# A streaming-encoder block on one core: k copied across partitions by GpSimd for two jobs, and six steps of the mixer put in another order

## What is computed

```python
proj = h @ w_in                       # q, k, v of 8 + 8 heads, gate, forget logits
o_sb = stick_breaking_attention(...)  # 8 heads of 64
o_fx = forgetting_attention(...)      # z = q k^T/8 + f_q - f_keys; softmax; @ v   (q, k RMS-normed)
o_sb = rmsnorm(o_sb); o_fx = rmsnorm(o_fx) * sigmoid(fox_gate)
mix  = concat([o_sb, o_fx]) @ w_out
x    = x + gate * mix
```

## Time and profile before

| | us |
|---|---|
| median of 3 runs | 1086.93 (1086.85 to 1087.13) |
| the profiled execution: time | 1086.3 |
| the profiled execution: span from first to last instruction | 1084.5 |

### The profile page before, as it was taken

One profiled execution on the slowest core, in us unless ns is written; L12 is line 12 of the kernel. 1 busy time (PEld: TensorE's weight loads), 2 busy tenths in 40 slices (PEclk: granted clock), 3 DMA queues, 4 the chain that ended last, 5 costly groups with the idle time before them and its releaser, 6 DMA issues.

```text
span 1084.5 us, 16281 instructions
## 1 busy us (share of the span) xinstructions
PE 1070.2 (99%) x6072; PEld 911.4 (84%) x6072; DVE 692.1 (64%) x1054; ACT 501.6 (46%) x834; POOL 42.3 (4%) x76
## 2 busy tenths in 40 slices
PE   8999999999999999999999999999999999999998
PEld 5788888888878889889778777789999999988886
DVE  3755555555653557886786677578776676684343
ACT  5523222222322225776796676458544544541322
POOL 1000000000000001111111011000000000000000
PEclk9999999999999999999999999999999999999999
DMA  9868888885474552397799677246786676232221
GB/s 343 240 216 289 263 277 290 268 307 161 134 229 137 167 168 78 89 218 170 177 193 187 135 146 165 61 123 156 191 218 173 172 203 183 81 108 98 88 97 78
DMA packets 209197, 191.84 MB, mean 177 GB/s; under 512 B 7676, under 2 KB 183916, under 8 KB 207084
## 3 DMA queue, kind: packets, MB, share of 16 engines
q1 hardware_dynamic: 201392, 146.59, 45.7%
q0 software_dynamic: 7424, 44.04, 16.2%
q10 hardware_dynamic: 316, 0.32, 0.1%
HBM read 186.74 MB, written 44.04 MB: 213 GB/s over the span
## 4 chain that ended last, share of the span: by engine, by line
PE 91%; ACT 3%; DMA 2%; DVE 2%; issue 1%; SPq 0%; POOL 0%; DVEq 0%; ACTq 0%
PE bank L897 28%; PE bank L899 27%; PE bank L898 27%; PE bank L1256 1%; PE bank L908 1%; PE bank L1228 1%; PE bank L1204 1%; DMA w_raw<-in_w_ffn_down_dram 1%; PE bank L1205 1%; PE bank L1291 1%; DMA x_nat<-in_x_dram 1%; ACT w_hi L1432 1%; DMA k_hh_b<-k_hh_b 0%; PE bank L934 0%; DMA k_hh_a<-k_hh_a 0%
## 5 line engine op out<-in xcount | busy, mean ns | idle before, releaser
L897 PE MATMUL bank<-h_hi,w_hi 128*128 128x512 f32 (+1 forms) x592 | 230.3, 389 | 0.1
L899 PE MATMUL bank<-h_hi,w_lo 128*128 128x512 f32 (+1 forms) x592 | 223.5, 378 | 0.0
L898 PE MATMUL bank<-h_lo,w_hi 128*128 128x512 f32 (+1 forms) x592 | 223.4, 377 | 0.0
L1939 DVE TENSOR_TENSOR w_lo<-w_raw,w_hi 128x1024 fp32r<-128x1024 f32 x97 | 118.7, 1225 | 155.9 <-ACT w_hi L1432 155.3
L1432 ACT ACTIVATE w_hi<-w_raw 128x1024 fp32r<-128x1024 f32 x97 | 102.5, 1057 | 203.8 <-PE bank L899 181.1
L897 PEld LDWEIGHTS bank<-h_hi,w_hi 128*128 128x128 f32 x592 | 111.8, 189 | 25.5 <-issue 4.2
L898 PEld LDWEIGHTS bank<-h_lo,w_hi 128*128 128x128 f32 x592 | 111.7, 189 | 24.0 <-issue 2.9
L899 PEld LDWEIGHTS bank<-h_hi,w_lo 128*128 128x128 f32 x592 | 111.6, 189 | 22.6
L2046 DVE TENSOR_TENSOR up_lo<-up_raw,up_hi 128x1024 fp32r<-128x1024 f32 x80 | 86.6, 1086 | 21.0 <-ACT up_hi L1502 21.0
L899 PE MATMUL bank<-combo,up_lo 128*128 128x256 f32 x320 | 90.6, 283 | 0.0
L897 PE MATMUL bank<-combo,up_hi 128*128 128x256 f32 x320 | 90.5, 283 | 0.0
(11 more groups left out here) (284 smaller groups left out, 2143.7 us busy)
## 6 DMA issues: line engine op xcount, KB each, us to landing
w_sums<-in_w_ffn_up_dram POOLq DMA_DIRECT2D x24, 1280.0 KB, 8.7
ada_w<-in_w_ada_dram SPq DMA_DIRECT2D x56, 512.0 KB, 3.9
w_raw<-in_w_ffn_up_dram SPq DMA_DIRECT2D x48, 512.0 KB, 6.9
up_raw<-w_sums SPq DMA_DIRECT2D x40, 512.0 KB, 5.5
w_raw<-in_w_in_dram SPq DMA_DIRECT2D x28, 512.0 KB, 4.6
w_sums<-w_sums POOLq DMA_DIRECT2D x8, 1280.0 KB, 10.0
up_raw<-in_w_ffn_up_dram SPq DMA_DIRECT2D x20, 512.0 KB, 4.1
down_raw<-in_w_ffn_down_dram SPq DMA_DIRECT2D x20, 512.0 KB, 3.6
```

The costliest lines, as they stand in the source:

```text
L897: mm(dst, wh, xh, start=start, stop=False, skip_group_check=skip)
L898: mm(dst, wh, xl, start=False, stop=False, skip_group_check=skip)
L899: return mm(dst, wl, xh, start=False, stop=stop, skip_group_check=skip)
L1939: v.tensor_tensor(w_lo[:, s, :], w_raw[:, r, :], w_hi[:, s, :].bitcast(F32), ALU.subtract)\
```

## The change

For jobs 6 and 7 `repeat_k` makes the two copies of k with GpSimd instructions instead of DMAs, and the scores wait for their own semaphore. Six pairs are added to AHEAD, which apply in this order. In the list of each engine this makes:

- `square 5` stands in front of `part 4` (ACT alone; part 4 is the output of job 2).
- `split 94` stands behind ACT's copy of `decay 6,1` and behind `unload 5,3` (ACT and DVE), in front of the first prep of job 6.
- ACT, around the start of job 7. Before: gate passes of evac 22, split 96, decay 7,1, unload 6,3, prep 7,0. After: decay 7,1, unload 6,3, gate passes of evac 22, split 96, prep 7,0.
- DVE at the same place. Before: evac 22 (sig), sum 6,4, split 96, unload 6,3, prep 7,0. After: sum 6,4, unload 6,3, evac 22, split 96, prep 7,0.
- `square 14` stands in front of the gate passes of evac 23 (ACT alone).

PE's own order is the same as before.

```diff
@@ AHEAD
     (("prep", 6, 1), ("scale", 11)),
+    (("square", 5), ("part", 4)),
+    (("split", 94), ("stat", 11)),
+    (("decay", 7, 1), ("evac", 22)),
+    (("evac", 22), ("scores", 7, 0)),
+    (("split", 96), ("prep", 7, 0)),
+    (("square", 14), ("evac", 23)),
@@ semaphores
+        k_again = sem("k_again")
@@ repeat_k(j), on gpsimd
                 pool.wait_ge(*k_made(j))
+                if j >= 6:
+                    g.tensor_copy(k_hh[j % 2][HD:P, 0, :], k_hh[j % 2][0:HD, 0, :].bitcast(F32)).then_inc(k_again, 1)
+                    g.tensor_copy(k_hh[j % 2][0:HD, 1, :], k_hh[j % 2][HD:P, 1, :].bitcast(F32)).then_inc(k_again, 1)
+                    return
@@ scores, on tensor
-                        pe.wait_ge(k_twice[j % 2], 32 * (j // 2 + 1))
+                        pe.wait_ge(*((k_twice[j % 2], 32 * (j // 2 + 1)) if j < 6 else (k_again, 2 * j - 10)))
```

## The result

| | before | after |
|---|---|---|
| median, us (5 executions each, side by side) | 1086.93 | 1091.73 (1090.96 to 1093.41) |
| the profiled execution: time / span | 1086.3 / 1084.5 | 1093.41 / 1091.6 |
| granted TensorE clock over the span | 0.999 | 0.996 |

The change makes the kernel slower by 4.8 us: ratio 1.0045, interval 1.0034 to 1.0056. Forecast were 1088.6, with a range up to 1090.2; the sign was right, the size outside the range.

The account below looks back on a forecast made before the run. PE, busy 99% of the span, was taken as the bound, so only its idle time counted. Terms -0.6 (square 5), +0.2 (job 6), +2.1 (job 7) gave +1.7 us: 1088.6 from the 1086.93 median, range 1084.0 to 1090.2.

Parts of the forecast that it names:

- the copies and the waits removed: Start of jobs 6 and 7: GpSimd copies take 0.6 us each, and PE's waits for k of 1.0 and 1.2 go.
- Square 5: Square 5 ahead of part 4 on ACT removes PE's wait for the square's result: -0.6 us, bounds 0 and 0.62.
- job 6's order: Split 94 behind decay 6,1 and unload 5,3 delays DVE's prep 6,0: +0.2 us in place of -1.0.
- the sentence on what would be had without the move: Job 6 with split 94 unmoved: prep 6,1 would start at 634.95 and values 5,1 0.37 us earlier.
- job 7's order: Start of job 7: moved steps make prep 7,0 2.66 us late and hold PE at turn 7,4: +2.1 us.
- the step that left DVE's hold out of the sum: Jobs 6 and 7: copies holding up DVE's low part of k, left to a rival because no row showed it.
- second and third rivals: Second: moves cost nothing, all three waits go, -2.8 us, chance 0.20. Third: PE loses only 0.75 in job 7, +0.35, chance 0.12.
- first rival: Jobs 6 and 7: GpSimd's copies hold up DVE, +0.6 us per job on top, +2.9 in all, 1089.8; chance 0.22.

Follow-up runs that it names:

- e5: Changed kernel with only square 5 ahead of part 4 kept, k repeated by DMA in all jobs; 1087.36 us, ratio 0.9989 to the kernel before.
- e1: Changed kernel with the six moved steps taken back, only the GpSimd copies kept; 1088.44 us, ratio 1.0009 to the kernel before.
- e6: Changed kernel with GpSimd's copies started after DVE's low part of k, and only the square 5 move kept; 1086.44 us, ratio 0.9979 to before.
- e3: Changed kernel with GpSimd's copies started only after DVE has made the low part of k; 1089.38 us, ratio 1.0017 to the kernel before.
- e8: The changed kernel run once more, unaltered, in the same rounds as e7; 1091.71 us, ratio 1.0026 to the kernel before.
- e7: Changed kernel with eight unused identity matmuls filling PE's wait ahead of turn 7,0; 1090.70 us, ratio 1.0021 to the kernel before.
- e9: Changed kernel with copies after DVE's low part of k, without the split 94 and square 14 moves; one execution, 1087.89 us beside 1088.43 before.

## Why the prediction was wrong

**Right: the copies and the waits removed.** 0.61 us for the first (forecast 0.6), both waits for k gone. Square 5 gained 0.76 in the stretch; forecast was 0.6, from the wait alone.

**Right: job 6's order.** Forecast +0.2 against before, measured +0.27 (20.58 to 20.85), which is no more than what the wait for k moves this stretch by (e5, 20.80); prep 6,0 at 3.80 us for 3.8. But the sentence on what would be had without the move (values 5,1 0.37 earlier) was wrong: e1 and e6 get 0.07 to 0.08, because stat 11 then waits 0.98 for f_keys behind split 94. So with the copies in place the move costs 0.35 (20.50 to 20.85) and not the 0.6 that the working gives (values 5,1 at 638.92 with the move, 638.69 - 0.37 = 638.32 without). I had followed DVE's chain and not the reader of PE's bank.

**Right: job 7's order.** Forecast +2.1, and 37.54 - 35.27 = +2.27 in e3, where nothing else disturbs it (+2.64 against e5's 34.90). Prep 7,0 at 7.24 for 7.2, ACT idle 1.48 for 1.5, waits at turns 7,0, 7,3 and 7,4. The second and third rivals fall with it.

**Failed: the step that left DVE's hold out of the sum.** "No row shows such a hold" was true of the trace of before, which has no reading GpSimd instruction beside a DVE one. It was taken as evidence against, and the rival got 0.22. Its mechanism and its price were right: the pair at 2.20 for 1.51, +0.68 and +0.69 for the forecast 0.6 a job. PE meets it as a wait of 0.34 for pt_lo each time (631.12 above, and 658.15). By the Trainium skill, SBUF — State Buffer, Who interferes with whom, a two-input DVE instruction and a GpSimd instruction reading SBUF exclude each other. e1 against e3 agree that they hold each other up: together 2.20 and 0.61 + 0.96, apart 1.51 and 0.61 + 0.61. They don't show a full exclusion: one after another the four would take 2.73, and they lay within 2.20. The hold's term, 1.4 us for the two jobs, is missing from the sum.

**Failed: a term that wasn't there at all, the clock.** The forecast gave PE two microseconds of idle at turn 7,0 and priced them as idle alone. Behind them the clock fell, and the matmuls of values 6,1 ran at the lower level: 39.00 - 37.54 = 1.46 us. That the cost is the clock's is shown by these rows. That the idle brings the fall is supported, not proven: the fall comes again in e8; e7, where the same wait is filled with work, has none in its profile, though its median is only 1.0 us lower; and six of nine idles of this length had a fall behind them, against none of thirteen shorter ones.

With both, the sum is -0.76 + 0.68 + 0.27 + 0.69 + 2.27 + 1.46 = +4.6; measured +4.8, and +3.8 in e8, where a part of the executions is without the fall. Either alone on top of the forecast's +1.7 would have stayed inside the range (1086.93 + 1.7 + 1.4 = 1090.0). The range's upper end, 1090.2, was called the first rival's value, which was 1089.8.

**Open.** Why the clock fell behind the 1.82 us in the profiles of the change, e8 and e9 and not in that of e3, whose PE does the same around that wait; and why in one profile it fell with no wait ahead of it. Within the change the fall seems to differ from one execution to the next too. No run here tells whether the 1.4 us of other waits in the copies' stretches has a part in it: e9 hasn't them, and fell.

## What to carry to other kernels

A wait at one matmul tells an upper bound of what it is worth: here 2.2 us of waits for k held 0.75 (0.6 against the profile of e5), because stats behind them were due to wait for ACT anyway, so walk each engine's list on past the wait, the banks' readers too. When a forecast puts microseconds of idle on PE, it owes a second term for the matmuls behind it at the lower clock, with a chance: 1.5 us here for 1.8 us of idle, in six of nine such idles, and nothing where PE would have waited again soon behind it (e9). Before work is given to GpSimd, look at what DVE does beside it: starting the copies 1.6 us later, beside pt_lo and prep instead of the pair, gave the 1.4 us back, and k still was there 2 us before PE asked for it.

## What the runs showed of the hardware

- A GpSimd copy of 64 by 512 fp32 elements from one half of the partitions to the other took 0.61 us alone. Beside DVE's pair, the second copy took 0.96 and the pair 2.20 instead of 1.51: each lengthened the other, by 0.35 and 0.69. Beside pt_lo (0.75) and prep (0.68), as in e3, both copies took 0.61.
- An idle of PE of 1.82 or 1.83 us at turn 7,0, with the clock at its upper level before it, was followed by matmuls at the lower level in three profiles (512 columns in 0.63 instead of 0.39 us in that of the change) and by none in a fourth. Over all 14 profiles that was so behind six of nine idles of 1.82 to 2.02 us and behind none of thirteen of 1.18 to 1.76 us; one fall, at 40 to 50 us, had no idle ahead of it.
